# Hyena filter constants loaded one stage ahead, and C's dot products spread over the whole of X's projection

## What is computed

```
for l in range(DEPTH):                       # DEPTH = 2
    p = modulate(rms_norm(x)) @ w_in[l]      # the combined projection: q, k, v, g, conformer, Hyena, gates
    x = x + mod[2] * mixer_block(p, s_f, s_b, rope, hyena_filters(L, lp), lp)
    x = x + mod[5] * peer_ffn(modulate(rms_norm(x)), peer_wq, peer_keys, peer_u, peer_v)
    ...                                      # the same for ctx, but not in the last layer

def hyena_filters(L, lp):
    h = sin(freq * (feat @ hy_w1 + hy_b1))
    h = sin(freq * (h @ hy_w2 + hy_b2))
    h = (h @ hy_w3 + hy_b3) * window         # L x 2 x 2 x 512
    return rfft(taps / norm(taps))

def expert_block(hb, eb, gb):                # peer_ffn: 128 picked experts for each token
    a = einsum('tkd,td->tk', u_tab[eb], hb)  # the dot products
    return einsum('tk,tkd->td', gelu(a) * gb, v_tab[eb])
```

## Time and profile before

| | us |
|---|---|
| median of 3 runs | 6275.75 |
| lowest and highest | 6272.06, 6276.57 |
| the profiled execution, its own time | 6281.48 |
| its span | 6279.7 |
| PE busy in the span | 5243.4 |
| DVE busy | 4242.6 |
| POOL busy | 854.5 |

### The profile page before, as it was taken

One profiled execution on the slowest core, in us unless ns is written; L12 is line 12 of the kernel. 1 busy time (PEld: TensorE's weight loads), 2 busy tenths in 40 slices (PEclk: granted clock), 3 DMA queues, 4 the chain that ended last, 5 costly groups with the idle time before them and its releaser, 6 DMA issues. The chain is left out here.

```text
span 6279.7 us, 70702 instructions
## 1 busy us (share of the span) xinstructions
PE 5243.4 (83%) x24102; PEld 4067.7 (65%) x24102; DVE 4242.6 (68%) x7449; ACT 1848.6 (29%) x3221; POOL 854.5 (14%) x644
## 2 busy tenths in 40 slices
PE   7787737788886677999999788978895659999998
PEld 5385636643355566889888647723473549999997
DVE  1347577748786687999999832368335986677666
ACT  0133211122012265333333211221021653333333
POOL 0000005500242000333333200000000001111110
PEclk8897868889898888999999889989997679999999
DMA  6141317711574256999999812201121247777775
GB/s 212 71 145 63 107 54 269 287 42 47 178 247 171 87 158 198 382 394 398 394 395 397 313 51 70 97 8 67 44 87 50 71 129 267 275 274 272 277 275 193
DMA packets 465495, 1180.22 MB, mean 188 GB/s; under 512 B 225436, under 2 KB 259645, under 8 KB 412543
## 3 DMA queue, kind: packets, MB, share of 16 engines
q1 hardware_dynamic: 373186, 641.52, 30.1%
q0 software_dynamic: 92160, 536.91, 22.4%
HBM read 1114.09 MB, written 64.23 MB: 188 GB/s over the span
## 5 line engine op out<-in xcount | busy, mean ns | idle before, releaser
L2025 POOL DMA_INDIRECT arena<-in_peer_uv,kept x384 | 518.9, 1351 | 3741.1 <-POOLq L1910 2105.2
L221 PE MATMUL psum<-h_hi,u_ring_hi 128*128 128x384 f32 x2048 | 693.6, 339 | 12.6 <-DVE ring_lo L2113 12.5
L221 PE MATMUL psum<-h_hi,ring_lo 128*128 128x384 f32 x2048 | 694.1, 339 | 0.0
L221 PE MATMUL psum<-h_lo,u_ring_hi 128*128 128x384 f32 x2048 | 693.4, 339 | 0.0
L221 PE MATMUL psum<-v_ring_hi,w_hi 128*128 128x512 f32 x1536 | 609.7, 397 | 6.4 <-DVE ring_lo L2118 6.4
L221 PE MATMUL psum<-ring_lo,w_hi 128*128 128x512 f32 x1536 | 603.8, 393 | 0.0
L221 PE MATMUL psum<-v_ring_hi,w_lo 128*128 128x512 f32 x1536 | 600.5, 391 | 0.0
L2118 DVE TENSOR_TENSOR ring_lo<-kept,v_ring_hi 128x1024 fp32r<-128x1024 f32 x256 | 313.8, 1226 | 299.2 <-ACT v_ring_hi L2073 294.1
L2157 DVE SCALAR_TENSOR_TENSOR arena<-arena 128x1024 f32<-128x1024 f32 x384 | 482.0, 1283 | 22.6 <-issue 5.7
L2145 DVE CUSTOM_DVE_ANT_0 arena<-arena 128x1024 f32<-128x1024 f32 x384 | 462.8, 1219 | 28.7 <-DMA arena<-in_peer_uv,kept 27.9
L2085 ACT ACTIVATE w_hi<-arena 128x384 fp32r<-128x384 f32 x256 | 134.7, 526 | 968.4 <-DVE arena L2128 968.4
(11 more groups left out here) (342 smaller groups left out, 10410.2 us busy)
## 6 DMA issues: line engine op xcount, KB each, us to landing
kept<-in_mix SPq DMA_DIRECT2D x312, 512.0 KB
kept<-in_peer_u SPq DMA_DIRECT2D x256, 512.0 KB
kept<-in_peer_uv SPq DMA_DIRECT2D x256, 512.0 KB
kept<-in_ada SPq DMA_DIRECT2D x96, 512.0 KB
gate_scratch<-arena SPq DMA_DIRECT2D x12, 4096.0 KB, 20.8
arena<-gate_scratch SPq DMA_DIRECT2D x128, 384.0 KB, 6.2
arena<-in_k_dft_x SPq DMA_DIRECT2D x6, 2048.0 KB
spec_scratch<-arena SPq DMA_DIRECT2D x4, 2048.0 KB, 8.5
```

Of the source, the lines that this page charges most:

```text
L221: done = pe.matmul(out, lhs[x], rhs[y], start=first and j == 0, stop=last and j == 2)
L2025: pool.indirect_dma_start(rows[q % NBUF], None, peer_uv, bass.IndirectOffsetOnAxis(ap=row_id[q % G][:, q // G:q // G + 1], axis=0))\
```

## The change

**Filters.** The weights, features, window and table get places of their own (`M0 + 33920` and on for the weights, `M0 + 36096` for the features) and three semaphores of their own (`filter_in`). For layer 0 the prologue loads the weights, both features, and C's window and table, behind its other loads. X's window and table use C's place, so `stage_filters(0, "X")` still loads these two at its start. For layer 1, SP loads all six in `stage_merge_experts(0)`, which had nothing on SP before.

**Dots.** `dots_of` is a list of shares: 24 dots over the 8 q/k blocks and 40 over the 8 v blocks as before, 24 over the g blocks, 26 over the glu blocks, and the last 14 (`LATE`) over the 12 hp blocks. Those 14 use two buffers in `tmp`'s place, and POOL begins their gathers when the last glu block has been taken out of PSUM. The hp blocks are written out one by one on DVE where the stage has dots, in place of a loop.

```diff
+            late = [area(m["ret"] + 1024 * k, D) for k in range(2)]
+            LATE = 14
+            EARLY = P - LATE
+            dots_of = shares(24, 8) + shares(40, 8, 24) + shares(24, 8, 64) + shares(EARLY - 88, 8, 88) + shares(LATE, 12, EARLY)
...
-                        gather_ctx(pool, peer_rows, bufs, 0, P)
+                        gather_ctx(pool, peer_rows, bufs, 0, EARLY)
+                        pool.wait_ge(bank_free.sem, bank_free.at(32 + 4))
+                        gather_ctx(pool, peer_rows, late, EARLY, P, EARLY)
...
-                            at = first + each * (4 * i + k)
-                            ctx_dots(dve, bufs, at, at + each)
+                            at, end = dots_of[first + 4 * i + k]
+                            if first < 32:
+                                ctx_dots(dve, bufs, at, end)
+                            else:
+                                ctx_dots(dve, late, at, end, EARLY, EARLY // len(bufs))
...
-                        skewed(dve, 12, rest(24), keep_hp, True, False)
+                        skewed(dve, 12, rest(24), with_dots(keep_hp, 32), True, False, beside)
...
+        def shares(total, parts, first=0):
+
+            at = [first + total * n // parts for n in range(parts + 1)]
+            return list(zip(at, at[1:]))
...
+        def load_filter_weights(sp, l):
+
+            at = M0 + 33920
+            sp.dma_start(area(at, HID)[0:EMB, :], hw1[l]).then_inc(filter_in[0].sem, 16)
+            sp.dma_start(area(at + 64, HID)[0:HID, :], hw2[l]).then_inc(filter_in[0].sem, 16)
+            sp.dma_start(area(at + 128, 2048)[0:HID + 1, :], hw3[l]).then_inc(filter_in[0].sem, 16)
...
+                load_filter_weights(sp, 0)
+                load_filter_features(sp, "C")
+                load_filter_features(sp, "X")
+                load_filter_tables(sp, "C")
                 sp.wait_ge(consts_in.sem, consts_in.at(80))
...
-                    sp.dma_start(feat[0:EMB, :], k_feat).then_inc(consts_in.sem, 16)
-                    sp.dma_start(w1[0:EMB, :], hw1[l]).then_inc(consts_in.sem, 16)
-                    sp.dma_start(w2[0:HID, :], hw2[l]).then_inc(consts_in.sem, 16)
-                    sp.dma_start(w3[0:HID + 1, :], hw3[l]).then_inc(consts_in.sem, 16)
-                    sp.dma_start(win.rearrange("p a b c -> p (a b c)"), k_win).then_inc(gates_in[0].sem, 16)
-                    sp.dma_start(dft.rearrange("p a b c -> p (a b c)"), k_dft[0]).then_inc(gates_in[1].sem, 16)
+                    if l == 0 and s == "X":
+                        load_filter_tables(sp, s)
...
-                    pe.wait_ge(consts_in.sem, consts_in.at(64))
+                    pe.wait_ge(filter_in[0].sem, filter_in[0].at(ready))
...
             with nc.Block() as block:
+                if l < DEPTH - 1:
+                    @block.sync
+                    def _(sp):
+                        load_filter_weights(sp, l + 1)
+                        load_filter_features(sp, "X")
+                        load_filter_tables(sp, "X")
```

More of the change, by code:

```diff
@@ L284, in build, with gather_ctx @@
         ctx_out = area(8192, D)
-        def gather_ctx(pool, table, bufs, first, end):
+        def gather_ctx(pool, table, bufs, first, end, freed=0):
             for q in range(end - first):
                 if q >= len(bufs):
-                    pool.wait_ge(ctx_free.sem, ctx_free.at(q - len(bufs) + 1))
+                    pool.wait_ge(ctx_free.sem, ctx_free.at(freed + q - len(bufs) + 1))
                 pool.indirect_dma_start(bufs[q % len(bufs)], None, table,
@@ L293, in gather_ctx, with ctx_dots @@
                     .then_inc(ctx_rows_in[q % len(bufs)].sem, 16)
-        def ctx_dots(dve, bufs, first, end):
+        def ctx_dots(dve, bufs, first, end, start=0, turns=0):
             for q in range(first, end):
-                k = q % len(bufs)
-                dve.wait_ge(ctx_rows_in[k].sem, ctx_rows_in[k].at(16 * (q // len(bufs) + 1)))
+                n = q - start
+                k = n % len(bufs)
+                dve.wait_ge(ctx_rows_in[k].sem, ctx_rows_in[k].at(16 * (turns + n // len(bufs) + 1)))
                 dve.tensor_tensor_reduce(bufs[k], bufs[k], ctx_h, 1.0, 0.0, ALU.mult, ALU.add, ctx_weight[:, q:q + 1])\
@@ L613, in _ @@
                                 j += 1
-            consts_in.add(64)
-            for c in gates_in:
+            if not (l == 0 and s == "C"):
+                filter_in[0].add(ready)
+            for c in filter_in[1:]:
                 c.add(16)
@@ L791, in _, with with_dots @@
                     hstep = T + 2
-                    def with_dots(keep, first, each):
+                    def with_dots(keep, first):
                         def finish(i, k):
                             keep(i, k)
-                            at = first + each * (4 * i + k)
-                            ctx_dots(dve, bufs, at, at + each)
+                            at, end = dots_of[first + 4 * i + k]
[3 more added lines that the diff above has]
+                                ctx_dots(dve, late, at, end, EARLY, EARLY // len(bufs))
                         return finish if beside else keep
@@ L807, in _ @@
                         dve.wait_ge(ctx_in.sem, ctx_in.at(32))
-                    skewed(dve, n_qk, rest(0), with_dots(keep_qk, 0, 3), False, False, beside)
+                    skewed(dve, n_qk, rest(0), with_dots(keep_qk, 0), False, False, beside)
                     if beside:
                         for n in range(8):
-                            with_dots(keep_v, 24, 5)(n // 4, n % 4)
+                            with_dots(keep_v, 8)(n // 4, n % 4)
                     else:
@@ L818, in _ @@
                         dve.memset(m["cp"][:, :, HALF + T:], 0.0)
-                        skewed(dve, 8, rest(8), with_dots(keep_g, 64, 4), False, True, beside)
-                        skewed(dve, 8, rest(16), with_dots(keep_glu, 96, 4), True, True, beside)
+                        skewed(dve, 8, rest(8), with_dots(keep_g, 16), False, True, beside)
+                        skewed(dve, 8, rest(16), with_dots(keep_glu, 24), True, True, beside)
                         dve.drain()
@@ L832, in stage_project @@
                 ctx_in.add(32)
-                counted_ctx(bufs, P)
+                counted_ctx(bufs, EARLY)
+                counted_ctx(late, LATE)
             act_a.add(KC)
```

23 lines of the change are left out of this document (17 added, 6 removed).

## The result

The changed kernel took 6249.07 us (median of 10 runs, 6236.37 to 6263.04), the kernel before 6290.39 (10 runs, 6272.06 to 6303.5): a ratio of 0.9944, 95% interval 0.9931 to 0.9957. That is 35 us by the ratio and 41 us by the two medians; the interval allows 27 to 43. Two repeats beside other runs of before gave 0.9931 (0.9915 to 0.9946) and 0.9927 (0.9902 to 0.9953), by their medians 45.6 and 44.9 us. The profiled execution took 6244.39 us, 37.1 less than the one shown of before.

A forecast was written before the change was run, and what follows sets the result against it. It took PE's wait for loads to bound the filter stages' heads, and DVE with its gathers g and glu. Filters 21.1 plus dots 25.6 gave 46.7 us off 6281.48, 6234.8, then 6229 at the runs' median; range 6221 to 6245.

The forecast's parts named there:

- Rival A: X's projection, g and glu: gathers stay the bound, the dots save only 11 to 18 us, time 6240; chance 0.20.
- C: Hp blocks: late gathers stop PE and the kernel gets slower, only from a gather time of 19.6 us; chance 0.01.
- D: Filters and dots: quick gathers and no stalls in glu, gains of 22 and 31 us, time 6223; chance 0.10.
- B: Filters: the wait is moved, not removed, losing 5 or more of 21.1 us, time 6234 to 6240; chance 0.08.
- the median of the runs is 5.7 lower, so the forecast is 6229: Whole run: 46.7 us off the profiled 6281.48 gives 6234.8, then lowered to the runs' median level.
- 7.6 + 8.0 less two starts: Layer 0's filter stages: waits of 7.6 (C) and 8.0 us (X) go; 0.4 us off all three filter stages for starts.
- Lands about 1 us later: Layer 1's modulation: the parameters' load finds the last tables ahead of it; cost 1.0 us, from 0 to 4.
- I cost this at nothing: Prologue: its seven filter loads, 2.2 MB in about 7 us, cost nothing, or 1 us if the cover fails.
- The cover that I named: Prologue: PE still has ring blocks in hand when the seven loads end near 24 us.
- 25.6 forecast: Dots in X's projection: 31.9 less 2.5 less 3.8 us gives a gain of 25.6, from 11 to 29.6.
- 101.1 + 2.5: First g copy to second hp copy: 101.1 us for 133.0 before, plus 2.5 us for late gathers.
- that term, 2.3 for 3.8: Hp: 3.8 us cost, from 2.3 for two end dots, 1.0 last gather, 0.5 sixth block; 2.3 by the page's fit.

The follow-up runs named there:

- before_again: The kernel before measured again as a control, nothing changed; ratio 0.9994 to the kernel before (0.9982 to 1.0006).
- filters_only: The changed kernel with X's projection as before, so only the filter loads moved; ratio 0.9956 to the kernel before.
- v36: The changed kernel with 36 dots in the v blocks for 40, 24 in glu for 26, 20 in hp for 14; ratio 0.9948 to the kernel before.
- rest_first: The changed kernel with the rest of g's first block ahead of the last v copy and its five dots; median 6233.62 us, ratio 0.9912 to the kernel before.

## Why the prediction was right and where it was wrong

**Direction and mechanism** were right: PE starts with each filter stage, g and glu are no longer bound by dots, hp has room for 14. Nothing ahead moved either: the first g copy came 119.7 us after the stage's start, and 120.3 before the change. Rival A falls (1.5 us of gather waits in g and glu, not above 5), C falls in the changed kernel, D too. B falls but for the 1.0 us that the forecast already had in its sum.

**The steps that failed.** The measured difference was 41.3 us of the 46.7 forecast, but 6249.07 is 20.1 above 6229 and outside the range. 14.6 of that are the base, set in the step "the median of the runs is 5.7 lower, so the forecast is 6229": 6275.75 stood there for a median of before that the ten runs put at 6290.39. 5.7 of the 14.6 come from going below the profiled execution's 6281.48, and 8.9 from that execution being itself below the median. The three runs of before, 6272.06 to 6276.57, lie at the low end: all 58 runs of before on record have a median of 6288.5 and go from 6271.84 to 6308.87. Six of the 58 are no higher than 6276.57; why the first three all were isn't shown. The range held the bounds of the terms and nothing for the base, though one stage wanders by 20 us. The other 5.4 are in the terms. The repeats gave 45.6 and 44.9 us, so the runs' times alone don't tell 5.4 from nothing; the terms below come from the table as differences of means:

- Filters, layer 0: 187.3 to 172.7 us, 14.6; forecast 7.6 + 8.0 less two starts, 15.3. At PE's start 15.5 were gained in the first pair of profiles, 0.7 went again within X's stage; I did not pursue that.
- Filters, layer 1: 125.0 to 118.4, 6.6; forecast 6.9 less a start.
- "Lands about 1 us later" for the parameters: 1.0. The rule of the Trainium skill ("DMA: Bandwidth & Descriptors", section "Queues, rings and completion order") gave the same, and the traces agree with it in the lateness: landing took 4.2 us for 2.6. No run tells waiting in order from sharing the engines.
- "I cost this at nothing", the prologue: 2.0 at PE's start. The cover that I named, PE's ring blocks, held; but the wait was for the constants ahead of the loads, which I had not looked at. The ring order of that section of the Trainium skill gives no reason for it, since the constants stand ahead, and the measurement decides: final_g took 14.7 us to land for 12.3 in the pair shown.
- Dots: 25.6 forecast. Against the profile of before that I worked from it was 310.3 - 284.0 = 26.3; against the mean of three (306.5 to 283.1, five profiles with the change's numbers of dots) 23.4. The trace that I worked from was the longest of the three: from the first g copy to the second hp copy 133.0 us, before_again 129.2, filters_only 126.0. Waits for gathers don't explain that (14.4, 15.8 and 14.6 us). PE's idle time (26.9, 24.9, 23.1) and its busy time for the same blocks (106.2, 104.2, 102.9, at a granted clock of 0.92, 0.95 and 0.96) do between them; what started it stays open.

14.6 + 6.6 - 1.0 - 2.0 + 23.4 = 41.6, and the medians say 41.3. That these agree so closely is partly luck, with repeats 4 us apart. Of the dots' parts: g copies came every 5.96 us for 5.85, the first g to the second hp copy took 105.0 for 101.1 + 2.5 (gather waits 1.5 for 2.5, but 14.2 us from the last glu copy to the second hp copy for 12.4); the stage ended 2.2 us later behind its last copy for 3.3; in hp nothing was lost at the sixth block (0.5 forecast) nor by the last gather (1.0 forecast), because a gather took 4.85 us there and not 7.74. The fit in the Trainium skill ("DMA: Bandwidth & Descriptors", section "Anatomy of one DMA — SWDGE (gpsimd) path"), 3.2 us by estimate, was below the measured gather. It is less than half of the 7.74 in the rows, but not of the 5.85, as the forecast had it. Its result for that term, 2.3 for 3.8, was still the better one, by luck: 4.85 us too is short enough for two buffers at one dot a block.

## What to carry to other kernels

Before a difference is taken from a time, measure how far the same kernel's runs and stages spread: here one stage wandered by 20 us, half of what this change gained, and three runs gave a median 15 us below that of ten. Work that is spread over more blocks is paced by its buffers as well as by the engine: count gather time + dot + hand-over per buffer, not DVE's sum. A load issued "early" is free only when nobody waits for what is already in flight, even if that stands ahead of it.

## What the runs showed of the hardware

- A 4 KB load issued ahead of seven others on SP's queue landed in 13.1 to 15.3 us with them behind it (nine profiles) and in 12.3 and 13.4 without (two).
- A gather of 512 KB took 4.85 us from issue to dot in a stretch with a DMA share of 0.64, where 7.74 was seen at 0.87; the second of two issued 2.0 us apart took 5.9 to 6.5 in v36, at 0.66.
- The same expert loop took 1103.1 to 1123.5 us in fourteen profiles, its bytes at 389 to 381 GB/s.
- With PE idle for 12.92 us before the first g block, the ten products behind the first took 0.63 us each where later ones take 0.40; the granted clock was 0.50, the lower of the two levels (1.2 GHz), from 1092 to 1097 and 0.99 from 1097 to 1099. After 6.50 us of idle time in rest_first it was the same: 0.50 for the first 4 us, and 1.00 (2.4 GHz) 6 us after the start.
